# Two token halves through the norm seams: the context half of the last output tile is made and normed before the latent half

## The chip, the cores and the metric

The kernel runs on one core of a Trainium2 chip. The metric is the device time of one execution in microseconds (us); three executions were timed, and one more was profiled. A difference of under 0.3% (8 us) can't be told from none.

## The reference, cut to what matters

256 latent and 256 context tokens of 1024 channels pass through two layers with the same weights. Each layer is SwiGLU, a token mixer (pooling, gated DeltaNet, attention), SwiGLU, and each of these starts with an RMS norm whose gain and shift differ between latent and context tokens.

```python
def rmsnorm(x, g, eps=1e-6):
    y = xf * lax.rsqrt(jnp.mean(xf * xf, axis=-1, keepdims=True) + eps)
    return (y * g.astype(F32)).astype(x.dtype)
def modulate(h, shift, scale):
    return h * (1.0 + scale) + shift
def ffn_sublayer(s, m, g_norm, w_in, w_out):
    h = modulate(rmsnorm(s, g_norm), m[0], m[1])
    return s + FFN_RES * m[2] * swiglu(h, w_in, w_out)
def trunk_layer(x, xc, mod, mod_c, p, ctx_out):
    mx = jnp.split(mod[:, None, :], N_MOD, axis=-1)
    mc = jnp.split(mod_c[:, None, :], N_MOD, axis=-1)
    x = ffn_sublayer(x, mx[0:3], p["norm_ffn1"], p["w_ffn1_in"], p["w_ffn1_out"])
    xc = ffn_sublayer(xc, mc[0:3], p["norm_ffn1"], p["w_ffn1_in"], p["w_ffn1_out"])
    x, xc = mixer_sublayer(x, xc, mx[3:6], mc[3:6], p, ctx_out)
...
```

## The kernel before, in words

Activations lie channel-major: `x` is 8 tiles of 128 channels by 512 tokens, columns 0 to 255 latent and 256 to 511 context. Every dense product in float32 is made of three fp32r matmuls (`products`, L1509 to L1511): upper part of the weights by upper part of the rows, upper by rest, rest by upper. Weight blocks of 128x1024 come by DMA into a ring of four slots (`load`, L418, on SP's queue, let go when TensorE counts the block four earlier in `s_pe`); ScalarE rounds them to `w_hi` (`cast`, L628) and VectorE makes `w_lo` as the difference (`lower`, L1023). Each engine runs an order that is written out by hand; semaphores alone join them, so a waiting instruction holds all that stands behind it on its engine.

The program has seven norm stages s = 0 to 6. Stages 1 and 4 open the mixers of layers 0 and 1, stages 2, 3 and 5 a SwiGLU, stage 6 the output. What the text calls a seam is the way from the last matmul of one sublayer to the steady run of the next:

- GpSimd sums the squares of tiles 0 to 6 as they are finished (`squares`, L510 and L511); VectorE adds the last product tile to `x` (`add_to_x`, L1029), ScalarE squares it (L643).
- TensorE sums over channels (L1495, L1496), ScalarE takes the root, VectorE the inverse (L998), and TensorE spreads it over the partitions (L1502).
- For each tile k VectorE scales (L1007), ScalarE shifts each half (L660) and rounds all 512 columns to `h_hi` (L664), and VectorE makes `h_lo` (L1015). Two buffers in `buf_a` and two in `buf_b` hold the way between.
- TensorE runs the first two blocks of the next product tile by tile as `h_lo` comes (`first_two`).

In a mixer (`mixer_pe`, `mixer_vec`, `mixer_act`) the small projection `ba` follows, 96 products of 16 columns (L1582 to L1584), and then projection blocks n = 2 to 15. The first six are taken from PSUM by ScalarE (`take`) and convolved by VectorE (`convolve`, L1151 to L1155). A SwiGLU (`ffn`) makes 44 blocks up and then eight output tiles of 22 k-steps, 66 matmuls each, in four chunks of weights (`down`). Between these VectorE computes modulation rows (`modulate`, L1055), for which GpSimd starts the loads. The mixer ends with eight output blocks of 24 matmuls.

## Time and profile before

| | us |
|---|---|
| median of 3 runs | 2613.21 (2607.35 to 2613.88) |
| profiled execution | 2612.21 |
| its span, first to last instruction | 2610.5 |
| TensorE (PE) busy | 2461.7 |
| VectorE (DVE) busy | 1404.3 |
| ScalarE (ACT) busy | 868.3 |
| GpSimd (POOL) busy | 217.9 |

Lines are those of the kernel before. "PE" are matmuls, "PEld" the loads of their weights, which run beside them. A matmul is shown longer than the step to the next, since they overlap; so the pace is read from the starts. "PEclk" is the granted clock of TensorE as a share of 2.4 GHz: 0.50 is the lower of its levels, 1.2 GHz.

### The profile page before, as it was taken

Reading aid. Unit: us, or ns where it says so; the run is one execution under the profiler, and the core shown is the slowest. Engines: PE = TensorE matmul, PEld = TensorE weight load, DVE = VectorE, ACT = ScalarE, POOL = GpSimd, SP = SyncE. Lnnn points to the kernel's source line nnn. Section 1 sums busy time; section 2 is a strip of 40 time slices with the busy share of each in tenths; the row PEclk is TensorE's granted clock in tenths of the full one; section 3 lists DMA queues with packets and bytes.
Section 4 is the critical chain, followed back from the end, with each engine's and each line's share of the span. In section 5 each row is a group of like instructions: output and inputs, shape, how many; then the busy total and the mean of one; then the engine's idle time right before and its main releaser. Section 6 shows DMA issues by size and latency. Waiting matters only on the chain.

```text
span 2610.5 us, 36014 instructions
## 1 busy us (share of the span) xinstructions
PE 2461.7 (94%) x13680; PEld 2071.9 (79%) x13680; DVE 1404.3 (54%) x2355; ACT 868.3 (33%) x1309; POOL 217.9 (8%) x284
## 2 busy tenths in 40 slices
PE   5999999999989998999999999999999899988998
PEld 4788877886588886778888778888787697878998
DVE  4778776424543435478873365542355524346554
...
GB/s 230 145 193 193 184 169 148 73 93 49 37 37 25 49 22 161 97 166 192 192 184 104 102 129 144 145 110 94 121 81 104 49 3 49 13 96 149 187 173 149
DMA packets 96454, 303.04 MB, mean 116 GB/s; under 512 B 10592, under 2 KB 17504, under 8 KB 95328
## 3 DMA queue, kind: packets, MB, share of 16 engines
q1 hardware_dynamic: 76912, 229.95, 27.0%
...
q10 hardware_dynamic: 720, 2.44, 0.3%
...
q14 instruction: 29, 0.24, 0.0%
...
## 4 chain that ended last, share of the span: by engine, by line
PE 87%; DVE 7%; ACT 3%; issue 2%; DMA 1%; POOL 1%; DVEq 0%; ACTq 0%; POOLq 0%; SPq 0%
PE ps L1509 22%; PE ps L1511 21%; PE ps L1510 21%; PE ps L1783 4%; PE ps L1792 4%; PE ps L1799 2%; PE ps L1687 2%; PE ps L1708 2%; DVE w_lo L1023 2%; PE ps L1475 1%; ACT buf_b L660 1%; PE ps L1837 1%; PE ps L1838 1%; PE ps L1696 1%; PE ps L1624 1%
## 5 line engine op out<-in xcount | busy, mean ns | idle before, releaser
L1509 PE MATMUL ps<-h_hi,w_hi 128*128 128x512 f32 (+1 forms) x2048 | 762.5, 372 | 38.4 <-DVE h_lo L1015 27.3
L1510 PE MATMUL ps<-h_lo,w_hi 128*128 128x512 f32 (+1 forms) x2048 | 742.7, 363 | 0.0
L1511 PE MATMUL ps<-h_hi,w_lo 128*128 128x512 f32 (+1 forms) x2048 | 742.6, 363 | 0.0
L1023 DVE TENSOR_TENSOR w_lo<-raw,w_hi 128x1024 fp32r<-128x1024 f32 (+2 forms) x416 | 476.2, 1149 | 490.7 <-ACT w_hi L628 485.8
L628 ACT ACTIVATE w_hi<-raw 128x1024 fp32r<-128x1024 f32 (+2 forms) x416 | 404.9, 975 | 688.1 <-DMA raw<-in_w_down 315.8
L1509 PEld LDWEIGHTS ps<-h_hi,w_hi 128*128 128x128 f32 x2048 | 394.7, 193 | 136.2 <-issue 66.5
L1511 PEld LDWEIGHTS ps<-h_hi,w_lo 128*128 128x128 f32 x2048 | 394.3, 193 | 58.8
L1510 PEld LDWEIGHTS ps<-h_lo,w_hi 128*128 128x128 f32 x2048 | 395.1, 193 | 54.5
L1509 PE MATMUL ps<-a_hi,w_hi 128*128 128x512 f32 (+1 forms) x960 | 348.7, 363 | 28.9 <-DVE a_lo L1421 16.3
L1511 PE MATMUL ps<-a_hi,w_lo 128*128 128x512 f32 (+1 forms) x960 | 349.5, 364 | 0.0
L1510 PE MATMUL ps<-a_lo,w_hi 128*128 128x512 f32 (+1 forms) x960 | 347.9, 362 | 0.0
L1055 DVE CUSTOM_DVE_ANT_0 ps<-ada,c_wide 128x1024 f32<-128x1024 f32 x256 | 319.4, 1248 | 8.1 <-DMA ada<-in_w_ada_t 2.9
L1509 PEld LDWEIGHTS ps<-a_hi,w_hi 128*128 128x128 f32 x960 | 183.6, 191 | 62.0 <-DVE a_lo L1421 16.9
L1510 PEld LDWEIGHTS ps<-a_lo,w_hi 128*128 128x128 f32 x960 | 183.4, 191 | 31.6
L1511 PEld LDWEIGHTS ps<-a_hi,w_lo 128*128 128x128 f32 x960 | 183.7, 191 | 29.0
L534 POOL DMA_DIRECT2D ada<-in_w_ada_t x128 | 68.1, 532 | 760.4 <-DVE ada_sum L1055 752.5
L680 ACT ACTIVATE a_hi<-buf_b 128x512 f32 (+3 forms) x88 | 51.0, 579 | 193.8 <-DVE buf_b L1041 193.8
L1783 PE MATMUL ps<-tm,amT 128*128 128x64 f32 x768 | 102.7, 299 | 5.7 <-ACT tm L886 5.7
L1783 PEld LDWEIGHTS ps<-tm,amT 128*128 128x128 f32 x768 | 101.6, 217 | 7.1 <-ACT tm L886 7.1
L898 ACT ACTIVATE um<-ps 128x256 f32<-128x256 f32 x96 | 31.8, 384 | 215.6 <-PE ps L1799 215.6
L1792 PE MATMUL ps<-xm,um 128*128 128x64 f32 x768 | 102.8, 299 | 0.0
L1792 PEld LDWEIGHTS ps<-xm,um 128*128 128x128 f32 x768 | 100.9, 216 | 0.0
...
## 6 DMA issues: line engine op xcount, KB each, us to landing
raw<-in_w_up SPq DMA_DIRECT2D x176, 512.0 KB, 4.0
ada<-in_w_ada_t POOLq DMA_DIRECT2D x128, 512.0 KB, 4.5
...
raw<-in_w_gate SPq DMA_DIRECT2D x48, 512.0 KB, 3.6
...
raw<-in_w_proj SPq DMA_DIRECT2D x32, 512.0 KB, 3.4
raw<-in_w_merge SPq DMA_DIRECT2D x16, 512.0 KB, 3.6
raw<-in_w_out SPq DMA_DIRECT2D x16, 512.0 KB, 3.4
```

Source lines behind the costliest of these rows:

```text
L534: pool.dma_start(ada[:, j, :], a["w_ada_t"][ADA_FIRST - KD + 2 * r + j]).then_inc(s_ada[j], 16)
L628: return act.activation(w_hi[:, j % RING, 0:cols], raw[:, j, 0:cols], ACT.Copy)
L1023: vec.tensor_tensor(w_lo[:, j % RING, 0:cols], raw[:, j, 0:cols], w_hi[:, j % RING, 0:cols].bitcast(F32), ALU.subtract).then_inc(s_lo, 1)
L1055: vec.tensor_tensor_reduce(ps[:, 6:8, :].rearrange("p b n -> p (b n)"), ada[:, j, :], c_wide[:, i, :], 1.0, 0.0, ALU.mult, ALU.add, ada_su ...
L1509: pe.matmul(out, wh, rows_hi[:, i, 0:n], start=first, stop=False)
L1510: pe.matmul(out, wh, rows_lo[:, i, 0:n], start=False, stop=False)
L1511: return pe.matmul(out, wl, rows_hi[:, i, 0:n], start=False, stop=last)
L1687: pe.matmul(ps[:, n % 2, keys], y[rows, 4 + t, cols], kT[rows, keys], start=True, stop=True).then_inc(sco.sem, 1)
L1708: ins = pe.matmul(ps[rows, 4 + n % 2, 0:P], v_nat[:, k, rows], probT[:, n % 2, k * P:(k + 1) * P], start=(k == k0), stop=(k == TT - 1))
L1783: ins = pe.matmul(ps[:, d, q * HD:(q + 1) * HD].rearrange("p (i c) -> p i c", c=b), amT[:, 8 * d + q, :], t, start=True, stop=True)
L1792: ins = pe.matmul(ps[:, d, q * HD:(q + 1) * HD], um[:, 8 * d + q, :], xm[:, 8 * d + q, :], start=True, stop=True)
L1799: ins = pe.transpose(ps[:, 2 + 2 * d + q // 4, (q % 4) * P:(q % 4 + 1) * P], tm[:, 8 * d + q, :], ident)
```

## The change

It touches stages 1 to 4, each now in two parts, context (p = 0) and then latent (p = 1), of 256 columns. Stages 0, 5 and 6 keep their code.

- **The tile before the norm.** The last output tile of a SwiGLU is made as a context half and then a latent half, 66 matmuls of 256 columns each. The sums of the context part stand 12 matmuls into the latent half, and its spread 15 matmuls further. Before stage 2 the last three output blocks (5, 6, 7) of the mixer are made for the context and then again for the latent tokens.
- **The norm.** ScalarE shifts in place (`shift`) in four slots, and rounds one step behind (`upper`). VectorE scales three tiles ahead (`scaled`) and makes `h_lo` (`rest`). Between them stand the weights of the next four blocks: 0 after tile 2 and 1 after tile 4 of the context part, 2 and 3 at its end. The latent add and square of the last tile stand after tile 4.
- **The first four blocks** (`first_four` for `first_two`) go into banks 0 to 3, first context columns and then latent ones, block 1 two tiles behind block 0. They are counted in `s_pe` only in the latent pass. In the mixers the `ba` projection now follows block 3 and not block 1, and the loops of `mixer_act` and `mixer_vec` round and lower weights only from n = 4 on.
- **Modulation.** Two rounds move from the down part of SwiGLU 0 to that of SwiGLU 2, and none stands beside the split tile.

Cut to its core (the helpers `part`, `part_cols`, `part_tiles`, `norm_slot` give the index, the columns, the 128-token tiles of a part, and the slot of a tile):

```diff
+SPLIT_STAGES = (1, 2, 3, 4)
+NORM_PARTS = (1, 2, 2, 2, 2, 1, 1)
+SPLIT_OUT = 5
-ADA_ROUNDS = (KF + KD, KF + 1, KF // 2)
-ADA_BASE = (0, KF + KD, 2 * KF + KD + 1)
+ADA_ROUNDS = (KF + KD - 2, KF + 1, KF // 2 + 2)
+ADA_BASE = (0, KF + KD - 2, 2 * KF + KD - 1)
...
+def proj_bank(n):
+    return n if n < RING else n % 2
+def out_bank(k, p):
+    return ((5, 0, 1), (2, 3, 4))[p][k - SPLIT_OUT]
...
+    def split_norm(s, l, which):
...
+        def shift(p, k):
+            c = part_cols(s, p, TOK)
+            act.wait_ge(s_t, KD * part(s, p) + k + 1)
...
+            act.activation(norm_slot(k)[:, c], norm_slot(k)[:, c], ACT.Identity,
+                           bias=mod[:, l, 3 * which * KD + k, 1 - p:2 - p],
+                           scale=gain[:, l, which, k, 1 - p:2 - p]).then_inc(s_act, 1)
+        def upper(p, k):
+            c = part_cols(s, p, TOK)
+            act.wait_ge(s_act, shifted[k])
+            act.activation(h_hi[:, k, c], norm_slot(k)[:, c], ACT.Copy).then_inc(s_hhi, 1)
+        last_square(0)
+        root(0)
+        act.wait_ge(s_mods, mods_at(l, which))
+        shift(0, 0)
+        for k in range(KD):
+            if k + 1 < KD:
+                shift(0, k + 1)
+            upper(0, k)
+            if k == 2:
+                weights(0)
+            if k == 4:
+                last_square(1)
+                weights(1)
+            if k == 6:
+                root(1)
+        weights(2)
+        weights(3)
+        shift(1, 0)
+        for k in range(KD):
+            if k + 1 < KD:
+                shift(1, k + 1)
+            upper(1, k)
...
+    def split_norm(s):
...
+        def scaled(p, k):
+            c = part_cols(s, p, TOK)
+            if k == 0:
+                vec.wait_ge(s_bc, part(s, p) + 1)
+            if k >= 4:
+                vec.wait_ge(s_h, KD * part(s, p) + k - 3)
+            vec.tensor_tensor(norm_slot(k)[:, c], x[:, k, c], ps[:, 6 + p, c], ALU.mult).then_inc(s_t, 1)
+        def rest(p, k):
+            c = part_cols(s, p, TOK)
+            vec.wait_ge(s_hhi, KD * part(s, p) + k + 1)
+            vec.tensor_tensor(h_lo[:, k, c], norm_slot(k)[:, c], h_hi[:, k, c].bitcast(F32),
+                              ALU.subtract).then_inc(s_h, 1)
+        if s == 2:
+            for k in range(SPLIT_OUT, KD):
+                add(0, k)
+        else:
+            add(0, KD - 1)
+        inverse(0)
+        if s == 2:
+            add(1, SPLIT_OUT)
+        for k in range(3):
+            scaled(0, k)
+        for k in range(KD):
+            rest(0, k)
+            if k + 3 < KD:
+                scaled(0, k + 3)
+            if k == 2:
+                if s == 2:
+                    add(1, SPLIT_OUT + 1)
+                lower(0, STAGE_BASE[s])
+            if k == 4:
+                add(1, KD - 1)
+                lower(1, STAGE_BASE[s] + 1)
+            if k == 6:
+                inverse(1)
+        lower(2, STAGE_BASE[s] + 2)
+        for k in range(3):
+            scaled(1, k)
+            if k == 0:
+                lower(3, STAGE_BASE[s] + 3)
+        for k in range(KD):
+            rest(1, k)
+            if k + 3 < KD:
+                scaled(1, k + 3)
...
         for n in range(N_PROJ + 3):
-            if n >= 2:
+            if n >= RING:
                 lower(n % RING, b0 + n)
             if n == 2:
...
-        for i in range(KD):
+        for i in range(KD if l else SPLIT_OUT):
             vec.wait_ge(s_pe, bo + i + 1)
-            add_to_x(i, 7 * (i % 2), no, l, 1).then_inc(outd.sem, 1)
+            add_to_x(i, 4 + i % 2, no, l, 1).then_inc(outd.sem, 1)
             if i + 3 < KD:
                 lower((i + 3) % RING, bo + i + 3)
...
+    def part_sums(s, p):
...
+    def part_spread(s, p):
...
+    def first_four(s, b):
+        lag = 2
+        for p in range(2):
+            c = part_cols(s, p, TOK)
+            def product(m, k):
+                return products(ps[:, m, c], h_hi, h_lo, m, k, k, c, k == 0, k == KD - 1)
+            pe.wait_ge(s_lo, b + 1)
+            for k in range(KD + lag):
+                if k < KD:
+                    pe.wait_ge(s_h, KD * part(s, p) + k + 1)
+                    ins = product(0, k)
+                if p and k == KD - 1:
+                    ins.then_inc(s_pe, 1)
+                if k == lag:
+                    pe.wait_ge(s_lo, b + 2)
+                if k >= lag:
+                    ins = product(1, k - lag)
+                if p == 0 and k == 4:
+                    part_sums(s, 1)
+            if p:
+                ins.then_inc(s_pe, 1)
+            else:
+                part_spread(s, 1)
+            for m in range(2, RING):
+                pe.wait_ge(s_lo, b + m + 1)
+                if p == 0 and s == 2:
+                    pe.wait_ge(outd.sem, outd.at(0, KD - 2 + m - 2))
+                for k in range(KD):
+                    ins = product(m, k)
+                if p:
+                    ins.then_inc(s_pe, 1)
...
+        i, s = KD - 1, (1, 3, 4)[f]
+        bd = b0 + 2 * KF + 4 * i
+        pe.wait_ge(s_down, KD * f + i - 2)
+        for m, (k0, k1) in enumerate(CHUNKS):
+            pe.wait_ge(s_lo, bd - 4 + m + 1)
+            for k in range(k0, k1):
+                ins = products(ps[:, 4, :], a_hi, a_lo, m, k - k0, k, TOK, k == 0, k == KF - 1)
+            ins.then_inc(s_pe, 1)
+        pe.wait_ge(s_down, KD * f + i - 1)
+        c = part_cols(s, 0, TOK)
+        for m, (k0, k1) in enumerate(CHUNKS):
+            pe.wait_ge(s_lo, bd + m + 1)
+            for k in range(k0, k1):
+                ins = products(ps[:, 5, c], a_hi, a_lo, m, k - k0, k, c, k == 0, k == KF - 1)
+        ins.then_inc(s_half, 1)
+        pe.wait_ge(s_down, KD * f + i)
+        c = part_cols(s, 1, TOK)
+        for m, (k0, k1) in enumerate(CHUNKS):
+            for k in range(k0, k1):
+                ins = products(ps[:, 4, c], a_hi, a_lo, m, k - k0, k, c, k == 0, k == KF - 1)
+                if k == 3:
+                    part_sums(s, 0)
+                if k == 8:
+                    part_spread(s, 0)
+            ins.then_inc(s_pe, 1)
...
-        first_two(MIX_STAGE[l], b0, TOK)
+        first_four(MIX_STAGE[l], b0)
...
+            dense(n, b0 + n, proj_bank(n), tok).then_inc(s_pe, 1)
             if 9 <= n < 12:
                 m = n - 2
```

VectorE in the norm of stage 1, context part, around the first two weight blocks of the mixer (L1177 is `scaled`, L1183 `rest`, L1142 the latent add of tile 7, L1222 `lower`), in the changed kernel:

```order
L1177 TENSOR_TENSOR buf_b<-x,ps 128x256 [waits h_ready]
L1222 TENSOR_TENSOR w_lo<-raw,w_hi 128x1024 [waits w_hi_ready]
L1183 TENSOR_TENSOR h_lo<-buf_b,h_hi 128x256 [waits h_hi_ready]
L1177 TENSOR_TENSOR buf_a<-x,ps 128x256 [waits h_ready]
L1183 TENSOR_TENSOR h_lo<-buf_a,h_hi 128x256 [waits h_hi_ready]
L1177 TENSOR_TENSOR buf_b<-x,ps 128x256 [waits h_ready]
L1142 SCALAR_TENSOR_TENSOR x<-ps,mod,x 128x256 [waits blocks_done]
L1222 TENSOR_TENSOR w_lo<-raw,w_hi 128x1024 [waits w_hi_ready]
L1183 TENSOR_TENSOR h_lo<-buf_b,h_hi 128x256 [waits h_hi_ready]
```

Both lowers were ahead of the norm before, behind the add of the last tile; now three and five tiles of the context part stand before them.

TensorE in the same place of the changed kernel, context pass of blocks 0 and 1:

```order
L1731 MATMUL ps<-h_hi,w_hi 128x256 [waits h_ready]
L1732 MATMUL ps<-h_lo,w_hi 128x256
L1733 MATMUL ps<-h_hi,w_lo 128x256
L1731 MATMUL ps<-h_hi,w_hi 128x256 [waits h_ready]
L1732 MATMUL ps<-h_lo,w_hi 128x256
L1733 MATMUL ps<-h_hi,w_lo 128x256
L1731 MATMUL ps<-h_hi,w_hi 128x256 [waits w_lo_ready]
L1732 MATMUL ps<-h_lo,w_hi 128x256
L1733 MATMUL ps<-h_hi,w_lo 128x256
L1731 MATMUL ps<-h_hi,w_hi 128x256 [waits h_ready]
L1732 MATMUL ps<-h_lo,w_hi 128x256
L1733 MATMUL ps<-h_hi,w_lo 128x256
```

Block 1 joins at tile 2 and waits there for its own weights, and all that follows on TensorE waits with it.

VectorE at the start of the mixer of layer 0, before (L1138 lowers the small weights, L1023 is `lower`, L1167 takes the `ba` projection, L1151 to L1155 are one convolution):

```order
L1138 TENSOR_TENSOR ba_lo<-ba_raw,ba_hi 128x128 [waits ba_hi_ready]
L1023 TENSOR_TENSOR w_lo<-raw,w_hi 128x1024 [waits w_hi_ready]
L1167 COPY ba<-ps 128x64 [waits ba_projected]
L1171 TENSOR_TENSOR gdt<-ba,ba_rows 128x32 [waits ba_taken,ba_rows_loaded]
L1151 TENSOR_SCALAR conv<-pre,vecs 128x512 [waits projection_taken]
L1153 SCALAR_TENSOR_TENSOR conv<-pre,vecs,conv 128x512 [waits vec_chain] x3
L1155 SCALAR_TENSOR_TENSOR conv<-pre,vecs,conv 128x512 [waits vec_chain]
L1023 TENSOR_TENSOR w_lo<-raw,w_hi 128x1024 [waits w_hi_ready]
L1151 TENSOR_SCALAR conv<-pre,vecs 128x512 [waits projection_taken]
```

and in the changed kernel (L1337, L1222, L1366 and L1350 to L1354 are the same operations):

```order
L1337 TENSOR_TENSOR ba_lo<-ba_raw,ba_hi 128x128 [waits ba_hi_ready]
L1366 COPY ba<-ps 128x64 [waits ba_projected]
L1370 TENSOR_TENSOR gdt<-ba,ba_rows 128x32 [waits ba_taken,ba_rows_loaded]
L1350 TENSOR_SCALAR conv<-pre,vecs 128x512 [waits projection_taken]
L1352 SCALAR_TENSOR_TENSOR conv<-pre,vecs,conv 128x512 [waits vec_chain] x3
L1354 SCALAR_TENSOR_TENSOR conv<-pre,vecs,conv 128x512 [waits vec_chain]
L1350 TENSOR_SCALAR conv<-pre,vecs 128x512 [waits projection_taken]
L1352 SCALAR_TENSOR_TENSOR conv<-pre,vecs,conv 128x512 [waits vec_chain] x3
L1354 SCALAR_TENSOR_TENSOR conv<-pre,vecs,conv 128x512 [waits vec_chain]
L1222 TENSOR_TENSOR w_lo<-raw,w_hi 128x1024 [waits w_hi_ready]
```

Before, a lower stood ahead of the wait for `ba_projected` and one behind the first convolution: blocks 2 and 3. Now the first lower behind that wait is block 4, and two convolutions stand ahead of it.

## Rows read from the trace of the kernel before

**Rows 1.** Windows: length, PE, PEld, DVE, ACT, POOL busy, PEclk, DMA share, GB/s.
```profile
436.50:446.38 9.88, 4.15 (x26) 3.68 (x25) 5.44 (x9) 4.77 (x8) 0.00 (x0) 0.69 0.52 173
446.38:459.36 12.98, 12.98 (x48) 10.48 (x49) 8.51 (x16) 11.15 (x23) 0.00 (x0) 0.84 0.24 81
459.36:475.27 15.91, 15.91 (x98) 15.91 (x96) 1.23 (x1) 2.48 (x4) 0.00 (x0) 0.65 0.18 67
475.27:489.08 13.81, 13.81 (x50) 11.15 (x50) 10.04 (x16) 3.46 (x4) 0.00 (x0) 0.78 0.11 38
1108.05:1143.92 35.87, 28.87 (x122) 23.15 (x121) 22.68 (x32) 25.08 (x37) 2.17 (x4) 0.86 0.35 120
1485.17:1523.07 37.90, 30.01 (x121) 24.11 (x121) 23.13 (x33) 23.28 (x36) 0.53 (x1) 0.82 0.20 62
1508.90:1512.10 3.20, 3.20 (x8) 2.13 (x7) 0.56 (x1) 1.73 (x2) 0.00 (x0) 0.50 0.02 5
1863.88:1916.88 53.00, 47.27 (x217) 41.42 (x217) 25.22 (x41) 21.86 (x36) 0.00 (x0) 0.74 0.25 82
1887.13:1903.94 16.81, 16.81 (x97) 16.81 (x96) 1.23 (x1) 2.47 (x4) 0.00 (x0) 0.61 0.18 63
```

**Rows 2.** Timeline of PE (start, length, line): 512-column products, down, then projection.
```profile
395.19 0.39 PE L1509 MATMUL ps<-a_hi,w_hi 128*128 128x512 f32 x1
...
414.09 0.39 PE L1509 MATMUL ps<-a_hi,w_hi 128*128 128x512 f32 x1
...
453.21 0.39 PE L1509 MATMUL ps<-h_hi,w_hi 128*128 128x512 f32 x1
...
458.67 0.40 PE L1509 MATMUL ps<-h_hi,w_hi 128*128 128x512 f32 x1
```

**Rows 3.** Timeline of PE, 256-column products and small sums, mixer of layer 1.
```profile
1959.76 0.28 PE L1509 MATMUL ps<-h_hi,w_hi 128*128 128x256 f32 x1
...
1961.20 0.95 PE L1573 MATMUL ps<-consts,buf_a 128*128 128x2 f32 x8
```

**Rows 4.** Groups by shape: busy us, mean ns, idle before.
```profile
L660 ACT ACTIVATE buf_b<-buf_a,mod,gain 128x256 f32<-128x256 f32 x88 | 48.0, 588 | 42.0 <-DVE buf_a L1007 42.0
L664 ACT ACTIVATE h_hi<-buf_b 128x256 fp32r<-128x256 f32 x8 | 3.3, 417 | 0.3
L628 ACT ACTIVATE w_hi<-raw 128x1024 fp32r<-128x1024 f32 x288 | 303.6, 1056 | 372.3 <-DMA raw<-in_w_up 313.5 <-DMA raw<-in_w_out 39.5 <-DMA raw<-in_w_proj 14.0
L1007 DVE TENSOR_TENSOR buf_a<-x,ps 128x256 f32<-128x256 f32 x16 | 6.5, 418 | 2.8 <-PE ps L1502 2.2 <-ACT out_t L654 0.6
L1023 DVE TENSOR_TENSOR w_lo<-raw,w_hi 128x1024 fp32r<-128x1024 f32 x288 | 352.4, 1227 | 318.7 <-ACT w_hi L628 315.4 <-DVE mod_rest L1060 1.9
```

**Rows 5.** Timeline of ACT in the norm of stage 1.
```profile
444.88 0.63 ACT L664 ACTIVATE h_hi<-buf_b 128x512 fp32r<-128x512 f32 x1
445.42 0.59 ACT L660 ACTIVATE buf_b<-buf_a,mod,gain 128x256 f32<-128x256 f32 x1
```

**Rows 6.** Timeline of PE in the seam of stage 3.
```profile
1507.60 0.50 PE L1509 MATMUL ps<-h_hi,w_hi 128*128 128x512 f32 x1 [2.15 <-DVE h_lo L1015]
```

**Rows 7.** Timeline of DVE after the small projection, mixer of layer 0.
```profile
475.45 0.23 DVE L1167 COPY ba<-ps 128x64 f32<-128x64 f32 x1 [13.79 <-PE ps L1584]
...
475.89 0.48 DVE L1151 TENSOR_SCALAR conv<-pre,vecs 128x512 f32<-128x512 f32 x1
...
478.77 0.75 DVE L1155 SCALAR_TENSOR_TENSOR conv<-pre,vecs,conv 128x512 f32<-128x512 f32 x1
```

**Rows 8.** Timeline of ACT, same place.
```profile
483.84 0.60 ACT L733 ACTIVATE pre<-ps 128x512 f32<-128x512 f32 x1 [22.00 <-PE ps L1511]
...
486.29 1.04 ACT L628 ACTIVATE w_hi<-raw 128x1024 fp32r<-128x1024 f32 x1
```

**Rows 9.** The page, DMA issues: KB each, us to landing.
```profile
raw<-in_w_proj SPq DMA_DIRECT2D x32, 512.0 KB, 3.4
```

**Rows 10.** Waits of PE from 489 to 720 us (total, times, longest).
```profile
PE ps L1708 <- ACT probT L855: 1.3, 2, 0.8
```

More of the change, by code:

```diff
@@ L380, in tile_ready, with part, part_cols, part_tiles @@
             return s_down, KD * {1: 0, 3: 1, 4: 2, 6: 3}[s] + k + 1
+        def part(s, p=0):
+            return sum(NORM_PARTS[:s]) + p
+        def part_cols(s, p, n):
+            return slice(0, n) if NORM_PARTS[s] == 1 else (slice(LAT, TOK), slice(0, LAT))[p]
+        def part_tiles(s, p, n):
+            c = part_cols(s, p, n)
+            return slice(c.start // P, c.stop // P)
+        def norm_slot(k):
+            return (buf_a, buf_b)[k % 2][:, k // 2 % 2, :]
+        def context_ready(s):
+            if s == 2:
+                return outc, KD - SPLIT_OUT
+            return s_addc, {1: 1, 3: 2, 4: 3}[s]
+        def proj_bank(n):
+            return n if n < RING else n % 2
+        def out_bank(k, p):
+            return ((5, 0, 1), (2, 3, 4))[p][k - SPLIT_OUT]
         def root_cols(l, i):
@@ L639, in casts @@
                         cast(j).then_inc(s_hi, 1)
+                if NORM_PARTS[s] == 2:
+                    return split_norm(s, l, which)
                 if 0 < s < 6:
@@ L1499, in norm @@
                     first_modulation()
[L1500 removed]
+                pe.wait_ge(s_inv, part(s) + 1)
                 for t in range(n // P):
@@ L1537, in up @@
                         dense(2 * j + m, b0 + 2 * q + m, 2 * j + m, n).then_inc(s_pe, 1)
-                first_two(s, b0, n)
-                up(1, 1)
+                if NORM_PARTS[s] == 2:
+                    first_four(s, b0)
+                else:
+                    first_two(s, b0, n)
+                    up(1, 1)
                 with pe.Fori(1, KF // 2) as it:
```

175 lines of the change are left out of this document (138 added, 37 removed).

## The prediction

> **What bounds the kernel now.** I read the page first, for the busy shares: TensorE is busy 94% of the span (the table above), VectorE 54% and ScalarE 33%. So time is lost or won where TensorE stands still, runs at its low clock, or is given more work. The windows of the seams come next [rows 1]. The reader is to see there that the norm of stage 1 costs a gap of 9.9 us (436.50 to 446.38), in which TensorE does only the small sums and the spread, and that the first two blocks then take 13.0 us at a mean clock of 0.84. The steady pace of a 512-column matmul is (458.67 - 453.21) / 24 = 0.2275 us in a projection, and (414.09 - 395.19) / 81 = 0.2333 us in a down tile (24 and 81 matmuls lie between those starts) [rows 2]; two blocks at that pace are 48 x 0.2275 = 10.9 us, so 2.1 us of the 13.0 are clock and small waits. Four blocks at pace are 21.8 us. Up to the start of block 4 the four seams that change hold, beyond these and the `ba` projection, 9.9 + 13.0 + 13.8 - 21.8 = 14.9 us in stage 1, 35.9 - 21.8 = 14.1 in stage 2, 37.9 - 21.8 = 16.1 in stage 3 and 53.0 - 16.8 - 21.8 = 14.4 in stage 4 [rows 1], 59.5 in all. That is all there is to win, and the question is what the new order puts in its place.
>
> **What a half costs on TensorE.** A 256-column matmul starts every (1961.20 - 1959.76) / 12 = 0.120 us [rows 3]. Two halves take 0.240 us in place of 0.2275 or 0.2333. With 66 + 96 products in stages 1, 3 and 4 and 72 + 96 in stage 2 this is 654 pairs, some 7.5 us more work in all; it is inside the sums below. The Trainium skill (TensorE: Matmul & The Clock Gate, Part 1) has steps of the column count over 2.4 GHz plus 2.5 ns; by that two halves would cost 654 x 2.5 ns = 1.6 us and the sum would come out 5.9 us lower. The rows show 13 ns a pair here, so they are taken.
>
> **The norm under the latent half.** Clock zero is the first matmul of the latent half of the last tile (stage 1; stages 3 and 4 have the same order). That half takes 66 x 0.120 = 7.9 us, and in it stand 8 small sums, 0.9 us (those at 1961.20 last 0.95 [rows 3]), and 4 spreads, 0.5 us: it ends at 9.3. The context add and square, some 0.45 us each like the 256-column rows of VectorE and ScalarE (0.418 and 0.417 [rows 4]), are done at 1.2, before the sums ask at 12 x 0.120 = 1.4, so TensorE doesn't wait. The sums end at 2.3; root and inverse are small and done at 3.1; the spread stands 15 matmuls behind the sums, at 4.1. VectorE's first scaling ends at 5.2 (0.418 [rows 4]). ScalarE then needs 0.588 and 0.417 us for shift and rounding of a tile [rows 4], but starts an operation 0.09 us before the last has ended (0.63 long, next after 0.54 [rows 5]): 0.50 + 0.33 = 0.83 us a tile. The first shift ends at 5.8, the second at 6.3, the rounding of tile 0 at 6.65, and tiles 1 and 2 follow, tile 2 a little later, as its shift waits for VectorE's rest between the scalings. The rounding of tile 2 ends at 8.4, the cast of block 0 (1.06) at 9.4, its lower (1.23) at 10.6. **TensorE starts block 0 at 10.7 and has waited 1.5 us.**
>
> It runs 9 matmuls, to 11.8, and asks for block 1. VectorE comes out of the lower at 10.5, does two rests and two scalings (0.34 apart), and the latent add only at 11.9 to 12.4; ScalarE squares until 12.8 and only then casts block 1, to 13.8; the lower ends at 15.0. **TensorE waits 3.3 us, to 15.15.** All of the rest of `first_four` stands behind this. After it I find no wait: the context pass ends at 21.2 (39 matmuls, sums, spread), blocks 2 and 3 at 27.0, their weights being lowered at 20.8 and 22.9; in the latent pass h_lo of tile 7 comes at 30.8 and is asked for at 31.3. Sum: 31.0 of matmuls (66 + 192 of 0.120), 2.7 of sums and spreads, 4.8 of waits = 38.5 us.
>
> **The clock.** In the old seams the low clock reaches into the blocks: 12.98 - 10.9 = 2.1 us. In the seam of stage 3 a wait of 2.15 us [rows 6] is followed within 1.4 us by a stretch at 0.50 (1508.90 to 1512.10 [rows 1]), the lower of the two levels; in its 3.2 us 8 matmuls pass, the work of 1.8, a loss of 1.4. The new seam has waits of 1.5 and 3.3 us with 1.1 us of work between. I take a loss of 1.8 us in each of the four, between 0 (it holds) and 2.9, the loss behind the `ba` projection: 13.81 - 10.9 [rows 1].
>
> **The mixers' second seam, which the change opens.** Before, the first 13.8 us behind the `ba` projection (blocks 2 and 3) needed nothing from VectorE but one lower behind the first convolution. Now block 4 stands there. From the start at 475.27: the copy of `ba` at 475.45, the first convolution from 475.89 to 479.52 (478.77 + 0.75) [rows 7]; ScalarE takes block 2, loads a table, and casts block 4, 486.29 + 1.04 - 483.84 = 3.5 us behind it [rows 8], so to 483.05; VectorE's second convolution, as long as the first, ends at the same time; the lower takes 1.23 and TensorE 0.1 to start: 484.4. **9.15 us of wait in each of stages 1 and 4**, and block 4 then starts at the low clock: 1.8 us as above (bounds 1.4 and 2.9). Behind it VectorE needs 1.2 + 3.6 us a block against 5.5 on TensorE, so it doesn't come again.
>
> **Stage 2.** The last three output blocks are done twice, 72 matmuls each way. The same chain gives 38.9 us, as the sums stand 6 matmuls later and two adds more stand in VectorE's queue; GpSimd's squares of the latent tiles run beside the first lower, for which I put 0.4: 39.3.
>
> **The rest** costs nothing. Casts and lowers are as many as before. Two modulation rounds more in the down part of SwiGLU 2 stand where VectorE has some 15 us a tile for 4 us of lowers and the add. GpSimd's row load there has no square behind it that is due. SP's loads for blocks 4 to 7 are let go only in the latent pass: block 0 is counted 6.8 us before block 4 is due, and load 3.4 [rows 9], cast 1.06 and lower 1.23 are 5.7, with the hidden product 6.4. If that cover goes, a SwiGLU pays what the load is late.
>
> **The sum**, from the first matmul of the tile that is split (of block 5 in stage 2) to block 4, all "before" from [rows 1, 2]:
> - Stage 1: before 15.4 (66 x 0.2333) + 9.9 + 13.0 + 15.9 + 13.8 = 68.0; after 7.9 + 38.5 + 1.8 + 15.9 + 9.15 + 1.8 = 75.05. Slower by 7.1.
> - Stage 4: before 15.4 + 53.0 = 68.4; after the same with 16.8 for `ba` = 75.95. Slower by 7.6.
> - Stage 3: before 15.4 + 37.9 = 53.3; after 7.9 + 38.5 + 1.8 = 48.2. Faster by 5.1.
> - Stage 2: before 16.4 + 35.9 = 52.3; after 8.6 + 39.3 + 1.8 = 49.7. Faster by 2.6.
>
> In all 7.0 us slower. The profiled execution took 2612.2, which becomes 2619.2; the median is 1.0 above it, so 2620.2 us.
>
> **The rivals.**
> - *The clock holds* through the first four blocks. For it: no single wait is as long as the old gap of 9.9. Against: one of 2.15 was enough [rows 6]. It gives 4 x 1.8 = 7.2 back: 2613.
> - *Faster: the mixers' wait is repaid.* If TensorE waited for something else later in the projection or the gates, the 18.3 us would be taken from there; it turns the result as soon as over 7 of them come back, and gives 2602 if all do. Against: from 489 to 720 us its longest wait in total is 1.3 us [rows 10]. What stands behind it is its own work.
> - *Slower by more*: the clock stays low as long as behind `ba` (2.9 in all six places, 6.6 us more), or block 1's chain and the loads of blocks 4 and 5 are each a microsecond later. That is 2627.
> - *The change doesn't do what it says*: the context sums hold the latent half up, as a square or GpSimd's sum of tile 6 comes late. Each microsecond counts four times; this goes with the case above.
>
> **How the numbers follow.** The forecast has 0.52 (2614 to 2626), the held clock 0.16, the repaid wait 0.07, slower by more 0.25. Over 0.3% is over 7.8 us, about what a measurement can tell from no change: 2605.4 and 2621.0. The forecast lies 0.8 below that limit, so it gives 0.28 to "same" and 0.24 to "slower"; with the others: faster 0.08, same 0.45, slower 0.47. The range takes the clock's bounds (-8 to +7) and 1 us a seam for the chains: 2608 to 2631.
>
> **What would show it.** In the profile after: first matmul of block 0 some 1.5 us and first of block 1 some 5.8 us after the latent half's end, the first waiting for `w_lo`; PEclk at 0.50 behind it; in both mixers a gap of 9 us behind the `ba` projection that ends with a lower; in stage 3 a way to block 4 shorter by 5. It is wrong if the gap behind `ba` is missing, or if TensorE waits for `h_lo` or the sums rather than for the weights.

## The result, and the profile after

| us | before | changed |
|---|---|---|
| median | 2605.64 (20 runs, 2597.67 to 2613.88) | 2611.22 (20 runs, 2608.38 to 2615.74) |
| profiled execution | 2612.21 | 2615.42 |
| its span | 2610.5 | 2613.8 |

The ratio is 1.0023, with a 95% interval of 1.0013 to 1.0033: the change costs 5.6 us, under the 0.3% that the prediction set as its limit of "same". The forecast was 2620.2 (2608 to 2631). The range held, the time is 9 us too high, and the case that had the largest chance, slower by over 0.3%, is not the one that came. The forecast had started from three runs of the kernel before, with a median of 2613.2; the median of all twenty is 2605.6.

The page of the changed kernel (busy us and share, the granted clock in forty slices, then two groups: busy us, mean ns, idle before and its releasers):

```profile
span 2613.8 us, 37326 instructions
...
PE 2455.5 (94%) x14334; PEld 2102.3 (80%) x14334; DVE 1409.8 (54%) x2423; ACT 872.1 (33%) x1349; POOL 216.9 (8%) x288
...
PEclk9999999799989899999999999999989979898999
...
L1731 PE MATMUL ps<-h_hi,w_hi 128*128 128x512 f32 (+1 forms) x2176 | 784.2, 360 | 56.8 <-DVE w_lo L1222 36.5
L1222 DVE TENSOR_TENSOR w_lo<-raw,w_hi 128x1024 fp32r<-128x1024 f32 (+2 forms) x416 | 474.5, 1144 | 478.8 <-ACT w_hi L679 474.7
```

TensorE is busy 6 us less than before while it has 654 instructions more, and the largest single cause of its standing still is now `w_lo` (36.5 us ahead of L1731), where it was `h_lo` (27.3 us ahead of L1509). The windows of the seams (length, PE, PEld, DVE, ACT, POOL busy, PEclk, DMA share, GB/s), stage 1 whole, then the weight waits and what follows them in stages 2, 3 and 4, the `ba` pass of stage 4 and the first matmuls behind its wait:

```profile
422.04:439.08 17.04, 17.04 (x144) 17.04 (x143) 7.04 (x19) 7.02 (x13) 2.78 (x2) 1.00 0.27 82
439.08:445.02 5.94, 1.61 (x13) 1.20 (x11) 4.32 (x9) 4.52 (x11) 0.00 (x0) 0.91 0.77 226
445.02:454.78 9.76, 9.76 (x47) 9.76 (x48) 2.52 (x5) 2.74 (x5) 0.00 (x0) 0.53 0.56 201
454.78:472.50 17.72, 17.72 (x151) 17.72 (x150) 7.41 (x20) 8.36 (x19) 0.00 (x0) 1.00 0.25 82
472.50:490.59 18.09, 18.09 (x97) 18.09 (x96) 0.00 (x0) 0.00 (x0) 0.00 (x0) 0.56 0.12 37
490.59:500.04 9.45, 0.36 (x2) 0.30 (x3) 8.59 (x14) 4.80 (x7) 0.00 (x0) 0.50 0.00 0
500.04:505.60 5.56, 5.56 (x13) 4.36 (x14) 5.38 (x8) 0.72 (x1) 0.00 (x0) 0.51 0.00 1
...
1123.51:1129.83 6.32, 1.61 (x13) 1.20 (x11) 4.89 (x9) 4.16 (x10) 3.92 (x5) 1.00 0.51 157
1129.83:1137.38 7.55, 7.55 (x52) 7.55 (x52) 2.52 (x5) 2.74 (x5) 0.00 (x0) 0.77 0.59 243
...
1497.77:1503.72 5.95, 1.62 (x13) 1.21 (x11) 4.33 (x9) 4.53 (x11) 0.00 (x0) 0.87 0.59 176
1503.72:1513.59 9.87, 9.87 (x51) 9.87 (x52) 2.52 (x5) 2.74 (x5) 0.00 (x0) 0.56 0.01 2
...
1873.64:1879.58 5.94, 1.61 (x13) 1.21 (x11) 4.32 (x9) 4.52 (x11) 0.00 (x0) 0.83 0.80 234
1879.58:1889.29 9.71, 9.71 (x52) 9.71 (x52) 2.52 (x5) 2.74 (x5) 0.00 (x0) 0.57 0.51 197
...
1906.65:1922.14 15.49, 15.49 (x97) 15.49 (x96) 0.00 (x0) 0.00 (x0) 0.00 (x0) 0.66 0.13 40
...
1931.59:1935.57 3.98, 3.98 (x10) 3.11 (x10) 3.84 (x6) 0.72 (x1) 0.00 (x0) 0.50 0.00 0
```

Stage 1 reads from top to bottom like the prediction's chain: both halves of the last tile with 8 sums and 4 spreads in 17.04 us (forecast 7.9 + 9.3); 5.94 us with two waits and 9 matmuls; 9.76 us at a mean clock of 0.53; the rest of the first four blocks at 1.00; the `ba` pass; a window of 9.45 us in which TensorE does nothing; and 13 matmuls at 0.51. The waits of stage 1 in total, count and longest:

```profile
PE ps L1731 <- DVE w_lo L1222: 13.4, 3, 9.1
```

Three waits, all for `w_lo`: 9.1 us behind `ba`, and 4.3 for the first two together (in starts, steps of 1.56 and 3.33 where 0.12 is due). None is for `h_lo`, none for the sums.

| first matmul of the split tile to block 4, with the low clock just behind it | before | forecast | measured |
|---|---|---|---|
| stage 1 | 68.0 | 75.05 | 78.0 + 2.6 = 80.6 |
| stage 2 | 52.7 | 49.7 | 49.7 |
| stage 3 | 53.3 | 48.2 | 50.3 |
| stage 4 | 68.4 | 75.95 | 75.0 + 1.9 = 76.9 |
| sum | 242.4 | 248.9 | 257.5 |

(Measured from starts in the timeline: 422.04 to 500.04, 1105.02 to 1154.75, 1480.73 to 1531.05, 1856.60 to 1931.59; before: 421.09 to 489.08, 1091.26 to 1143.92, 1469.77 to 1523.07, 1848.48 to 1916.88. The 2.6 and 1.9 are the last windows above against 13 and 9 matmuls of 0.2275 [rows 2].) The seams cost 15.1 us more than before, but the span is only 3.3 longer. **Some 12 us came back where the change touches nothing.** Between the seams both kernels take the same time within 0.3 us (from block 4 of one to the split tile of the next 602.2, 325.9 and 325.4 us before; 602.4, once the 2.6 of the table is taken off, 326.0 and 325.6 now), so moving the modulation rounds cost nothing. What came back is behind stage 4, nearly all of it in one place: layer 1's first DeltaNet scan. There TensorE waits for `vnew` in both kernels, first before, then changed:

```profile
2172.71 0.40 PE L1837 MATMUL ps<-q_dec,state 64*64 64x128 f32 x2 [1.31 <-DVE vnew L1376]
```
```profile
2187.18 0.40 PE L2128 MATMUL ps<-q_dec,state 64*64 64x128 f32 x2 [1.29 <-DVE vnew L1575]
```

and the 35 us from that matmul on are, in the same order:

```profile
2172.71:2207.71 35.00, 35.00 (x200) 26.74 (x200) 9.98 (x34) 5.59 (x9) 1.96 (x4) 0.61 0.18 56
```
```profile
2187.18:2222.18 35.00, 30.39 (x255) 25.02 (x255) 20.76 (x66) 7.80 (x14) 1.96 (x4) 1.00 0.25 73
```

The instructions are the same and the wait is the same, 1.3 us. Before, the clock is at its lower level (0.50, 1.2 GHz, all through 2175 to 2200 us) for most of the stretch, mean 0.61, a clock loss of 0.39 x 35 = 13.7 us; in the changed kernel it stays at 1.00 and TensorE even has time to spare (30.39 of 35.00 busy), so less than the 13.7 shows as time. What shows is read from the same matmul at the end of the stretch, before and then changed:

```profile
2207.70 0.39 PE L1509 MATMUL ps<-h_hi,w_hi 128*128 128x256 f32 x1
```
```profile
2210.76 0.39 PE L1731 MATMUL ps<-h_hi,w_hi 128*128 128x256 f32 x1
```

It comes 35.0 us behind the wait before and 23.6 now: the changed kernel was 14.5 us late at the wait and is 3.1 late here, so 11.4 us are won in this stretch. Another 2 us had come back between block 4 and the wait.

### The profile page after: what moved, and what is told of

Its sections match the earlier page's. It is cut to its first block, busy times and chain, and to the rows that moved or that the text cites. A ratio compares the mean times of both kernels' runs of the same rounds, so it can differ in the third digit from the quotient of the medians.

```text
span 2613.8 us, 37326 instructions
## 1 busy us (share of the span) xinstructions
PE 2455.5 (94%) x14334; PEld 2102.3 (80%) x14334; DVE 1409.8 (54%) x2423; ACT 872.1 (33%) x1349; POOL 216.9 (8%) x288
## 4 chain that ended last, share of the span: by engine, by line
PE 86%; DVE 7%; ACT 3%; issue 2%; DMA 1%; POOL 1%; DVEq 0%; ACTq 0%; SPq 0%; POOLq 0%
PE ps L1731 22%; PE ps L1733 21%; PE ps L1732 21%; PE ps L2074 4%; PE ps L2083 4%; PE ps L2090 2%; DVE w_lo L1222 2%; PE ps L1978 2%; PE ps L1999 2%; PE ps L1674 1%; PE ps L1987 1%; PE ps L2128 1%; PE ps L2129 1%; ACT w_hi L679 1%; PE ps L1915 1%
## 5 line engine op out<-in xcount | busy, mean ns | idle before, releaser
L1731 PE MATMUL ps<-h_hi,w_hi 128*128 128x512 f32 (+1 forms) x2176 | 784.2, 360 | 56.8 <-DVE w_lo L1222 36.5
L1733 PE MATMUL ps<-h_hi,w_lo 128*128 128x512 f32 (+1 forms) x2176 | 764.5, 351 | 0.0
L1732 PE MATMUL ps<-h_lo,w_hi 128*128 128x512 f32 (+1 forms) x2176 | 764.5, 351 | 0.0
L1222 DVE TENSOR_TENSOR w_lo<-raw,w_hi 128x1024 fp32r<-128x1024 f32 (+2 forms) x416 | 474.5, 1144 | 478.8 <-ACT w_hi L679 474.7
L1731 PEld LDWEIGHTS ps<-h_hi,w_hi 128*128 128x128 f32 x2176 | 419.9, 193 | 147.5 <-issue 51.7
L1733 PEld LDWEIGHTS ps<-h_hi,w_lo 128*128 128x128 f32 x2176 | 420.0, 193 | 52.7
L1732 PEld LDWEIGHTS ps<-h_lo,w_hi 128*128 128x128 f32 x2176 | 420.6, 193 | 48.7
L1731 PE MATMUL ps<-a_hi,w_hi 128*128 128x512 f32 (+1 forms) x1050 | 365.7, 348 | 30.3 <-DVE a_lo L1620 16.3
L1731 PEld LDWEIGHTS ps<-a_hi,w_hi 128*128 128x128 f32 x1050 | 200.9, 191 | 59.0 <-DVE a_lo L1620 16.9
L1732 PEld LDWEIGHTS ps<-a_lo,w_hi 128*128 128x128 f32 x1050 | 201.0, 191 | 26.8
L1733 PEld LDWEIGHTS ps<-a_hi,w_lo 128*128 128x128 f32 x1050 | 200.5, 191 | 26.0
```

Source lines behind the costliest of these rows:

```text
L1222: vec.tensor_tensor(w_lo[:, j % RING, 0:cols], raw[:, j, 0:cols], w_hi[:, j % RING, 0:cols].bitcast(F32), ALU.subtract).then_inc(s_lo, 1)
L1731: pe.matmul(out, wh, rows_hi[:, i, c], start=first, stop=False)
L1732: pe.matmul(out, wh, rows_lo[:, i, c], start=False, stop=False)
L1733: return pe.matmul(out, wl, rows_hi[:, i, c], start=False, stop=last)
```

## The experiments

Medians below stand beside the kernel before on the same chip, which had medians of 2605.5 to 2607.6.

**Both kernels again.** No edit.

> The kernel before, unchanged, timed against itself. Theory A (the clock outside the seams falls differently from execution to execution): ratio 1.000, single times spread over some 8 us, and in its profile the stretch of layer 1's DeltaNet part that ran at a granted clock of 0.74 (2150 to 2200 us in the first profile) has another value, with a span that differs by as much as these stretches do. Rival B (the 13 us that the changed kernel got back behind stage 4 belong to the change): this stretch shows 0.74 again and the span is 2610 to 2611 again.

Measured 2606.13 (12 runs, 2594.37 to 2614.76), ratio 0.9997 (0.9978 to 1.0016). The 35 us behind the `vnew` wait:

```profile
2169.49:2204.49 35.00, 35.00 (x224) 27.56 (x225) 12.67 (x43) 5.59 (x9) 1.94 (x4) 0.71 0.19 57
```

Mean 0.71, a clock loss of 10.2 us instead of 13.7. The profiled execution is 5.5 us shorter in its span, of which this stretch gives 2.9; 3.2 lie ahead of it, mostly in the seams of stages 3 and 4 (52.2 and 66.5 us in place of 53.3 and 68.4), and 0.6 are lost again behind it. The single times of these twelve lie at 2594 to 2598 with a mean granted clock of 0.958 to 0.959 over the span, and at 2605 to 2615 with 0.950 to 0.953. With more runs the space between fills (8 of the 20 above lie from 2601 to 2605), so this is one wide spread rather than two groups.

> The changed kernel, unchanged. Theory A: ratio 1.002 to 1.003; the seams read as in its first profile (78.0 us in stage 1, 50 in stages 2 and 3, 75.0 in stage 4, each within 1 us), while the clock of the DeltaNet stretches behind stage 4 differs from the first profile. Rival B: those stretches read 1.00 and 1.00 again, as in its first profile.

Measured 2612.85 (12 runs, 2608.52 to 2616.81), ratio 1.0031 (1.0019 to 1.0043). The same stretch:

```profile
2185.91:2220.91 35.00, 30.39 (x255) 25.02 (x255) 20.76 (x66) 7.79 (x14) 1.96 (x4) 1.00 0.26 73
```

1.00 again, as in the first profile. The seams: 75.2 us in stage 1, where the first four blocks lost 2.7 us less to the clock than in the first profile, and 75.0 in stage 4. From the `vnew` wait to the matmul at the end of the stretch this pair of profiles differs by 8.5 us. So both theories had a part: the kernel before varies at this place (0.61 and 0.71), though neither profile has it at 1.00, and the changed kernel's 1.00 is no accident of one profile, as B says.

**The wait for `ba` moved.** In `mixer_vec`:

```
-                    if n == 2:
+                    if n == 5:
                         vec.wait_ge(bap.sem, bap.at(l, 1))
```

> The changed kernel with one thing moved: VectorE waits for the ba projection behind the third convolution and the lowers of blocks 4 and 5, and not ahead of them. Theory W (the wait of 9.1 us behind ba is VectorE's chain of ba copy, two convolutions and a lower, and nothing stands behind it that takes its time over): both gaps vanish, the low clock behind them too (2.6 and 1.9 us), so 18.2 to 22.7 us less than the changed kernel, 2589 to 2593 us, a ratio to the kernel before of 0.993 to 0.995. Rival R (TensorE waits for something else later, as the head sums or the gates): the gaps vanish and the time falls by less than 10 us, with new waits behind block 4. Rival C (the gap ends with the load of block 4): the gap shrinks to no less than 3 us.

Measured 2593.8 (12 runs), ratio 0.9971 (0.9949 to 0.9994): 19.0 us under the changed kernel. VectorE's timeline, the lowers of blocks 4 and 5 and the copy of `ba`:

```profile
471.87 1.22 DVE L1222 TENSOR_TENSOR w_lo<-raw,w_hi 128x1024 fp32r<-128x1024 f32 x1
...
476.55 1.22 DVE L1222 TENSOR_TENSOR w_lo<-raw,w_hi 128x1024 fp32r<-128x1024 f32 x1
486.18 0.22 DVE L1366 COPY ba<-ps 128x64 f32<-128x64 f32 x1 [8.40 <-PE ps L1875]
```

and the windows of the `ba` pass and of the first 9 matmuls of block 4:

```profile
470.63:485.99 15.36, 15.36 (x98) 15.36 (x97) 6.90 (x9) 3.27 (x5) 0.00 (x0) 0.68 0.13 41
485.99:489.87 3.88, 3.88 (x10) 3.07 (x11) 3.16 (x7) 0.00 (x0) 0.00 (x0) 0.52 0.01 2
```

The lowers are done 8 us before the pass ends (477.77 against 485.99), and block 4 starts with its last instruction: both gaps of 9.45 us are gone. The gaps alone are 18.9 of the 19.0, so nothing behind them takes its time over, and R and C fall. (The two profiled executions differ by more, 26.0 us, of which 22.7 are in the seams: here the `ba` pass of stage 1 is 2.9 us shorter besides. The median has slower executions in it.) What stays is the low clock behind `ba` (3.88 us for 9 matmuls, a loss of 1.8): it comes from the pass itself, not from the gap. Three of the twelve runs are at 2608 to 2611, with a granted clock of 0.953 to 0.954 against 0.959 to 0.962 in the others; no such run was profiled, so where they lose it is not known.

**Only the SwiGLUs' seams split.** `NORM_PARTS`, and guards so that the mixers run as before:

```
-NORM_PARTS = (1, 2, 2, 2, 2, 1, 1)
+NORM_PARTS = (1, 1, 2, 2, 1, 1, 1)
...
-            return n if n < RING else n % 2
+            return n if n < RING and NORM_PARTS[MIX_STAGE[l]] == 2 else n % 2
```

> Only the norms of stages 2 and 3 (the SwiGLUs') are split; stages 1 and 4 (the mixers') are as in the kernel before. Theory by stages: the two split seams win 2.9 and 3.0 us, and nothing is lost elsewhere, so 6 us less than the kernel before, ratio 0.9977 (0.997 to 0.9985); against the changed kernel 12 us less. Rival D (the seams' effects don't add up, the rest of the program answers with clock): the ratio is 1.000 or above.

Measured 2595.17 (12 runs, 2592.77 to 2597.93), ratio 0.9967 (0.9955 to 0.9979): 10.5 us under the kernel before where 6 were expected, 17.7 under the changed kernel. The two seams read 49.8 and 50.3 us, 5.9 us less than before together, as expected. In the DeltaNet stretch this kernel's clock was 0.90, a clock loss of 3.5 us against 10 to 14 in the kernel before's two profiles, enough for the other 4.6. The figure of 12 against the changed kernel was added up wrongly: by its own stage table the two mixer seams are worth 12.6 + 8.5 = 21. Rival D falls: the split of stages 2 and 3 is a gain, that of 1 and 4 the loss.

**Weights of blocks 0 and 1 earlier.** In ScalarE's and VectorE's `split_norm`:

```
-                    if k == 2:
+                    if k == 1:
                         weights(0)
+                    if k == 2:
+                        weights(1)
                     if k == 4:
                         last_square(1)
-                        weights(1)
```

and `lower(0, ...)` and `lower(1, ...)` moved the same way.

> The changed kernel with the casts and lowers of blocks 0 and 1 earlier in the context pass (behind tile 1 and tile 2, where they stood behind tile 2 and tile 4, and block 1's now ahead of the latent add and square). Theory W (the waits of 1.5 and 3.3 us are ScalarE's and VectorE's order, and each microsecond of them is on the path): the first shrinks to 0.5 to 0.7, the second to 0.5 to 1.5, so 2.6 to 3.8 us less in each of four seams, 10 to 15 us in all, 2598 to 2603 us. Clock theory C (the low clock of 4.2 us a seam comes from these waits): the clock holds besides, and it is up to 14 us more, 2584 to 2590. Rival L (the loads of blocks 0 and 1 are what ends the waits): they shrink by less than 0.5 us and the time stays within 3 us of the changed kernel's 2612.

Measured 2599.55 (12 runs), ratio 0.9977 (0.9961 to 0.9993), 13.3 us under the changed kernel. Waits in stage 1 up to the `ba` pass (total, count, longest), and the 6.5 us from block 1's first matmul:

```profile
PE ps L1733 <- DVE w_lo L1224: 1.2, 2, 0.8
```
```profile
439.38:445.87 6.49, 6.13 (x48) 5.84 (x48) 4.20 (x10) 4.65 (x10) 0.00 (x0) 1.00 0.68 230
```

The two weight waits fall from 4.3 to 1.2 us together (steps of 0.62 and 1.09 in place of 1.56 and 3.33), some 3 us a seam, and the granted clock behind them is 1.00 in all four seams. The waits were an order of two queues, not a load. The seams of its profile are 22.8 us shorter than in the first profile of the changed kernel, as W and C together ask; but the DeltaNet stretch had fallen to 0.71 again, and from the `vnew` wait to the matmul at its end 8.5 us of the gain were lost. So a gain in the seams was in part paid back there.

**Matmuls of no use in the weight waits.** In `first_four`, context pass only:

```
+                    def fill(count, rows):
+                        for _ in range(count if p == 0 else 0):
+                            pe.matmul(ps[:, 5, 0:LAT], rows[:, 0, LAT:LAT + P], rows[:, 0, LAT:TOK],
+                                      start=True, stop=True)
+                    fill(11, a_hi)
                     pe.wait_ge(s_lo, b + 1)
...
+                            fill(24, h_hi)
                             pe.wait_ge(s_lo, b + 2)
```

> The changed kernel, with 11 and 24 extra 256-column matmuls of no use put into the two weight waits of each split seam (1.3 and 2.9 us at 0.12 us each, in place of waits of 1.5 and 3.3). TensorE's order and the weights' chain stay. Theory C (the low clock behind the waits costs 4.2 us in stages 1, 3 and 4 and 1.9 in stage 2, and TensorE's stand is its cause): granted clock 1.00 through the first four blocks, 10 to 14.5 us less than the changed kernel, about 2599. Rival S (the small-sum matmuls or the load of the whole chip set the clock, not the stand): the clock falls all the same and the time is that of the changed kernel or up to 2 us more.

Measured 2609.05 (12 runs), ratio 1.0022 (1.0006 to 1.0038): 3.8 us under the changed kernel, where 10 to 14.5 were expected. Block 1's start to the spread, and the `ba` pass, stage 1:

```profile
444.77:450.44 5.67, 5.67 (x48) 5.67 (x49) 2.52 (x5) 2.75 (x5) 0.00 (x0) 1.00 0.66 215
...
468.15:485.59 17.44, 17.44 (x97) 17.44 (x96) 0.00 (x0) 0.00 (x0) 0.00 (x0) 0.58 0.11 35
```

What took 9.76 us takes 5.67 at a clock of 1.00, and the same in the other three seams; this shows the price of the low clock there, 4.1, 1.9, 4.2 and 4.0 us in the first profile. Theory C holds for the seams, S falls. Yet the whole program gained little. Against the first profile of the changed kernel the seams are 13.1 us shorter in all and the span 9.4 (2604.4); the difference is the DeltaNet stretch:

```profile
2173.19:2208.19 35.00, 34.43 (x253) 28.00 (x254) 16.57 (x55) 6.71 (x11) 1.94 (x4) 0.85 0.24 73
```

0.15 x 35 = 5.2 us of clock lost, where the changed kernel loses none, and 4.4 us later at the matmul at its end. The median gained less than this profiled execution (2606.14), and what the others lost no profile shows.

**Late `ba` wait and early weights together.** Both edits above.

> Late wait for ba and early weights together. If both act on different waits of the path they add: 19 us of the first and 10 to 15 (to 29 with the clock) of the second, so 2578 to 2584 us, or 2565 where the clock holds; a ratio to the kernel before of 0.985 to 0.992. Rival: the second shows no more than half of what it gives alone, as the seams' clock was low anyway.

Measured 2576.9 (5 runs, 2575.13 to 2584.92), ratio 0.9895 (0.9877 to 0.9913), and once more, beside the last kernel of this section:

> Late wait for ba and early weights once more, beside the version with the extra matmuls: 2577 (2575 to 2585); where its profile shows no low clock in layer 1's first DeltaNet scan, its time is under 2578.

2582.37 (6 runs, 2570.43 to 2586.0), ratio 0.9893 (0.9871 to 0.9914). The two edits add: 19.0 + 13.3 = 32.3 us under 2612.85 by the runs of each alone, 36 and 30.5 measured. In its two profiles the four seams take 25 to 27 us less than in the first profile of the kernel before, the mixers' 63 to 64 us where they took 67 to 68: with the weights and the `ba` wait moved, the split pays there too. Both of its profiled executions (2584.92 and 2581.85) have the low clock behind the `vnew` wait, here the first, and its runs spread over 16 us:

```profile
2145.94:2180.94 35.00, 35.00 (x200) 26.68 (x200) 10.06 (x34) 5.59 (x9) 1.93 (x4) 0.61 0.18 54
```

**Late `ba` wait and the fillers together.**

> Late wait for ba together with the extra matmuls. By theory C 2593.8 - 10 to 14.5 = 2579 to 2584 us; by rival S 2594 or more. If the clock of the ba pass is set by the stand ahead of it rather than by its own small matmuls, the pass falls from 15 to 18 us to some 12, another 6 us less in all.

Measured 2582.15 (6 runs), ratio 0.9916 (0.9898 to 0.9933), 11.7 us under the late wait alone: here the clock's price in the seams (13.1 us by the profiles) shows nearly in full, and the DeltaNet stretch of its trace is at 1.00. The `ba` pass still takes 17.2 and 16.9 us; its low clock is its own.

**Is the DeltaNet stretch the cause of the spread?** In the kernel before, ahead of the wait for `vnew`:

```
+                        if (l, w, t) == (1, 0, 1):
+                            for _ in range(10):
+                                pe.matmul(ps[:, 5, 0:LAT], h_hi[:, 0, 0:P], h_hi[:, 0, 0:LAT], start=True, stop=True)
                         pe.wait_ge(vn.sem, vn.at(l, n + 1))
```

> The kernel before, with 10 extra 256-column matmuls of no use in one place: layer 1's first DeltaNet scan, step 1, ahead of the wait for vnew (1.31 us in its trace, behind which the clock fell to 0.50 for some 25 us). Theory A (whether the clock falls at this wait differs from run to run, and this makes the kernel before's spread of 2594 to 2614 and the two profiles' loss of 13.7 and 10.2 us against none in the changed kernel's): the clock stays at 1.00 from 2170 to 2205 us, the median falls by 5 to 10 us to 2596 to 2600, and the upper half of the runs (2605 and above) disappears. Rival B (the fall has another cause, such as the stretch of small matmuls itself): the same median of 2606 or 1 us more, the same spread.

Measured 2597.94 (9 runs, 2593.02 to 2604.65), ratio 0.9972 (0.9957 to 0.9987). The ten matmuls fill the wait, and the 35 us behind them are at full clock:

```profile
2166.38 1.36 PE L1833 MATMUL ps<-h_hi 128*128 128x256 f32 x10
2167.75 0.43 PE L1840 MATMUL ps<-q_dec,state 64*64 64x128 f32 x2
```
```profile
2167.75:2202.75 35.00, 30.40 (x254) 25.00 (x255) 20.63 (x66) 7.73 (x14) 1.96 (x4) 1.00 0.23 72
```

The median is 9.7 us lower, for 1.2 us of useless work inside a wait, and no run over 2605 is left. Rival B falls: small matmuls alone don't bring the low clock here, it takes the wait of 1.3 us. Of theory A the place and the price hold. That the clock falls only in some executions of the kernel before is not shown, since both of its profiles have it; for it speaks the mean clock over the span, 0.958 here, 0.952 and 0.953 in those two profiles, and 0.958 to 0.959 in the runs of the kernel before at 2594 to 2598. And the spread stays: 11.6 us in these nine runs, 14.3 in the fifteen of the kernel before beside them, both ends of it 6 to 8 us lower. Most of the spread comes from elsewhere.

> The changed kernel with the same 10 extra matmuls in layer 1's first DeltaNet scan. Theory P (in the changed kernel the clock nearly always holds there by itself, so that it got back what the kernel before loses there in most runs, and this is why 15 us more in the seams showed as 6): the median stays within 2 us of 2611 to 2613, ratio to the kernel before 1.001 to 1.004. Rival Q (its two profiles were chance, it falls there as often as in the kernel before): the median falls by 5 to 10 us, ratio 0.998 to 1.000.

Measured 2614.37 (12 runs, 2609.76 to 2617.73), ratio 1.0032 (1.0019 to 1.0046), no less than without the matmuls. Its stretch behind the filled wait reads as it does without:

```profile
2187.80:2222.80 35.00, 30.39 (x255) 25.02 (x256) 20.84 (x67) 7.87 (x14) 1.96 (x4) 1.00 0.25 73
```

The changed kernel has nothing to lose there, as P says. The account by the two pairs of profiles: 15.1 and 15.9 us more in the seams, 11.4 and 8.5 less behind the `vnew` wait, less than a microsecond net elsewhere, and spans 3.3 and 6.8 longer. By the medians 5.6 remain, and the 9.7 of the filled wait is what the seams' 15 lack.

**The best of them.** Late `ba` wait, early weights, and the ten matmuls, on the changed kernel.

> Late wait for ba, early weights and the 10 extra matmuls of the DeltaNet scan together, on the changed kernel. By theory A no run of it lies near the 2585 of that version's profile (which lost 13.6 us there), median 2573 to 2577, ratio to the kernel before 0.987 to 0.989. By rival B the same as without them, 2577 to 2580.

Measured 2573.22 (4 runs, 2568.42 to 2576.21), ratio 0.9871 (0.9852 to 0.989): 34.4 us under the kernel before, so it beats both of the kernels of this case. It is 9.2 under the same kernel without the ten matmuls, run beside it, but only 3.7 under that kernel's first five runs, on another chip, and the intervals of the ratios overlap: with four runs, what the ten matmuls add here is not settled. Its slowest run, 2576.21, is where A had it, and its stretch is at 1.00.

## Why the prediction was partly right and why its number was wrong

Three steps failed: the base it started from, the clock's price in the new seams, and "the rest costs nothing". The waits themselves, which are the mechanism, came as forecast.

- **The norm under the latent half: right.** "TensorE starts block 0 at 10.7 and has waited 1.5", then 3.3: in the timeline the last matmul of the latent half starts at 439.08, block 0 at 440.64, and block 1 stands 3.33 behind the matmul ahead of it, each less 0.12 of work. The order was right too: ScalarE casts block 1 behind the latent square, and VectorE's lower ends the wait. The context sums hold nothing up: both halves of the last tile run in 17.04 us without a gap, which settles the rival that they would.

```profile
438.28 1.04 ACT L679 ACTIVATE w_hi<-raw 128x1024 fp32r<-128x1024 f32 x1
...
442.34 0.42 ACT L734 ACTIVATE buf_b<-x 128x256 f32<-128x256 f32 x1 [1.42 <-DVE x L1142]
442.67 1.04 ACT L679 ACTIVATE w_hi<-raw 128x1024 fp32r<-128x1024 f32 x1
```
```profile
439.36 1.23 DVE L1222 TENSOR_TENSOR w_lo<-raw,w_hi 128x1024 fp32r<-128x1024 f32 x1 [0.19 <-ACT w_hi L679]
...
441.83 0.48 DVE L1142 SCALAR_TENSOR_TENSOR x<-ps,mod,x 128x256 f32<-128x256 f32 x1
443.74 1.23 DVE L1222 TENSOR_TENSOR w_lo<-raw,w_hi 128x1024 fp32r<-128x1024 f32 x1 [1.43 <-ACT w_hi L679]
```

  (ScalarE, then VectorE: cast of block 0; square and cast of block 1; lower of block 0, latent add, lower of block 1.)

- **The mixers' second seam: right.** Forecast 9.15 us, measured 9.1 (a step of 9.45 with the last small matmuls' 0.36), by the chain that was named: copy of `ba`, two convolutions, cast, lower.

```profile
490.99 0.22 DVE L1366 COPY ba<-ps 128x64 f32<-128x64 f32 x1 [26.52 <-PE ps L1875]
...
491.43 0.48 DVE L1350 TENSOR_SCALAR conv<-pre,vecs 128x512 f32<-128x512 f32 x1
...
497.85 0.75 DVE L1354 SCALAR_TENSOR_TENSOR conv<-pre,vecs,conv 128x512 f32<-128x512 f32 x1
498.67 1.23 DVE L1222 TENSOR_TENSOR w_lo<-raw,w_hi 128x1024 fp32r<-128x1024 f32 x1
```

  Moving one wait took it away and brought all of it, which also settles the rival that it would be repaid: with nothing of the gap left, 19.0 us were gained, so nothing had repaid it.

- **What a half costs: nearly right.** A 256-column matmul takes 0.120 us (78 in 9.36). The prediction put 13 ns on every pair; against 0.2275 it is 12.5 ns, but against the down tiles' 0.2333 only 6.7. The 270 pairs that replace `a_hi` products cost 1.8 us and the 384 others 4.8, 6.6 in all for 7.5. The sums by stage had used 0.2333 in stages 1, 3 and 4 and so were not touched; in stage 2 they put 16.4 us before for 72 matmuls that also run at 0.2333, 16.8, so the seam took 52.7 before and the gain there is 3.0 us, not 2.6.

- **The clock: the term that was mis-sized.** "I take a loss of 1.8 us in each of the four, between 0 and 2.9." It was 4.1, 1.9, 4.2 and 4.0 in the first profile, 7.0 us more in all (in the second, stage 1 lost 1.4); the kernel with fillers shows it, with 5.67 us for the same stretch. The estimate rested on [rows 6], a single wait of 2.15 us; the new seam has two waits with 1.1 us of work between, and the clock stayed low through all of the 33 matmuls and eight sums that followed. The rest of the stage table's gap is the `ba` pass of stage 1 (18.1 against 15.9), its 2.6 behind it instead of 1.8, and stage 4's pass, 1.3 less than put.

- **"The rest costs nothing": wrong.** No instruction outside the seams changed its cost, and still 11.4 and 8.5 us moved there in the two pairs of profiles, because TensorE's clock answered differently to one wait of 1.3 us in the middle of small matmuls. The prediction had read the kernel before's trace as fixed outside the seams. It holds a stretch of 35 us at a mean clock of 0.61 that the changed kernel runs at 1.00: a term of minus 8 to 11 us that stood at nothing in the sum.

- **The base: wrong.** "The median is 1.0 above it" rested on three runs, 2613.21, 2607.35 and 2613.88, all from the upper half of a spread that reaches down to 2594. Against its own profile the forecast was +7.0, measured were +3.2 by the two profiles and +5.6 by the medians; against the median of twenty runs the same forecast reads as +14.6. Of the nine microseconds by which 2620.2 is too high, 7.6 stand in the base and 1.4 in the effect by the medians. That the effect came so near is luck: two errors stand against each other, 8 us too little in the seams and 12 not expected elsewhere. So is it that the range held.

What stays open is why the clock holds behind the `vnew` wait in both profiles of the changed kernel, and by the last test in nearly all of its executions, and falls in both of the kernel with late `ba` wait and early weights. The instructions and the wait there are the same; the time at which TensorE comes there is not. No run varies that time alone.
